# adaLN sums of a hybrid GLA / differential-attention step: groups of blocks in one PSUM bank with one turn each, four blocks per GLA head

## The reference, cut to what matters

```python
def adaln(cond, w, b):                       # w: (1024, 6144), one per layer
    m = jax.nn.silu(cond) @ w + b
    return [t[..., None, :] for t in jnp.split(m, 6, axis=-1)]

for i in range(DEPTH):                       # DEPTH = 2; GLA in layer 0, diff attention in layer 1
    mp = adaln(c_ctx, w_ada[i], b_ada[i])    # for the 128 context tokens
    ms = adaln(c, w_ada[i], b_ada[i])        # for the 512 latent tokens
    hs = rmsnorm(xs, g_mix_norm[i]) * (1 + ms[1]) + ms[0]
    # ... mixer, output os_
    xs = xs + ms[2] * os_
    hs = rmsnorm(xs, g_ffn_norm[i]) * (1 + ms[4]) + ms[3]
    xs = xs + ms[5] * swiglu(hs, w_ffn_gate[i], w_ffn_up[i], w_ffn_down[i])
```

## Time and profile before

| | us |
|---|---|
| median of 3 runs | 1852.03 |
| lowest and highest run | 1846.36, 1852.61 |
| the profiled execution | 1850.31 |
| its span, first to last instruction | 1848.5 |
| TensorE busy | 1745.5 (94%) |
| VectorE busy | 845.4 (46%) |
| ScalarE busy | 704.3 (38%) |
| GpSimd busy | 92.0 (5%) |

### The profile page before, as it was taken

The page is one execution under the profiler, slowest core; times in us unless marked ns, Lnnn a source line. Parts: engine busy times, 40 slices in busy tenths (PEclk is TensorE's granted clock), DMA queues, the critical chain, the costliest instruction groups (busy, mean ns, idle before and its releaser), DMA issues.

```text
span 1848.5 us, 28144 instructions
## 1 busy us (share of the span) xinstructions
PE 1745.5 (94%) x11618; PEld 1632.3 (88%) x11618; DVE 845.4 (46%) x1339; ACT 704.3 (38%) x1055; POOL 92.0 (5%) x139
## 2 busy tenths in 40 slices
PE   5999999979999999999989999996899999999997
PEld 2787787759999999999978999995899999999996
DVE  3434343445444323444356667775464432344433
ACT  5634344324322211222255777776252221122222
POOL 1101021010000000000000000000000000000000
PEclk8999999989999999999989999997999999999998
DMA  9234252332333323323213212222122222222321
GB/s 341 89 128 141 77 196 82 101 109 77 115 114 115 90 70 104 119 75 87 73 43 89 74 55 74 72 57 70 57 69 68 76 89 74 65 72 68 90 69 57
DMA packets 230627, 170.58 MB, mean 92 GB/s; under 512 B 8739, under 2 KB 214982, under 8 KB 229510
## 3 DMA queue, kind: packets, MB, share of 16 engines
q1 hardware_dynamic: 216742, 121.41, 22.4%
q0 software_dynamic: 13792, 47.85, 7.6%
HBM read 160.32 MB, written 4.72 MB: 89 GB/s over the span
## 4 chain that ended last, share of the span: by engine, by line
PE 86%; DVE 5%; ACT 4%; issue 2%; SPq 1%; DMA 1%; POOL 0%; DVEq 0%; ACTq 0%
PE acc L553 71%; PE side L600 2%; PE side L724 2%; PE side L959 2%; PE side L1004 1%; PE work L931 1%; PE acc L1004 1%; DVE state L1726 1%; SPq L378 1%; PE work L741 1%; DVE h_lo L1839 1%; DVE w_lo L1568 1%; PE work L694 1%; ACT w_hi L1077 1%; DMA a_first_x<-in_w_ada_dram 1%
## 5 line engine op out<-in xcount | busy, mean ns | idle before, releaser
L553 PE MATMUL acc<-h_hi,w_hi 128*128 128x320 f32 (+1 forms) x2432 | 584.8, 322 | 27.8 <-DVE h_lo L2087 10.4
L553 PE MATMUL acc<-h_lo,w_hi 128*128 128x320 f32 (+1 forms) x2432 | 559.5, 311 | 0.0
L553 PE MATMUL acc<-h_hi,w_lo 128*128 128x320 f32 (+1 forms) x2432 | 559.2, 311 | 0.0
L553 PEld LDWEIGHTS acc<-h_hi,w_hi 128*128 128x128 f32 x2432 | 410.6, 191 | 60.1 <-issue 34.5
L553 PEld LDWEIGHTS acc<-h_hi,w_lo 128*128 128x128 f32 x2432 | 413.4, 190 | 0.0
L553 PEld LDWEIGHTS acc<-h_lo,w_hi 128*128 128x128 f32 x2432 | 412.4, 190 | 0.0
L1077 ACT ACTIVATE w_hi<-w_raw 128x1024 fp32r<-128x1024 f32 (+1 forms) x184 | 204.1, 1109 | 375.3 <-PE acc L553 369.7
L1568 DVE TENSOR_TENSOR w_lo<-w_raw,w_hi 128x1024 fp32r<-128x1024 f32 (+1 forms) x184 | 237.9, 1293 | 227.6 <-ACT w_hi L1077 225.7
L553 PE MATMUL acc<-hid_lo,w_hi 128*128 128x320 f32 x704 | 160.3, 309 | 0.0
L553 PE MATMUL acc<-hid_hi,w_hi 128*128 128x320 f32 x704 | 160.3, 309 | 0.0
L553 PE MATMUL acc<-hid_hi,w_lo 128*128 128x320 f32 x704 | 160.3, 309 | 0.0
(11 more groups left out here) (271 smaller groups left out, 1747.3 us busy)
## 6 DMA issues: line engine op xcount, KB each, us to landing
a_raw<-in_w_ada_dram POOLq DMA_DIRECT2D x80, 512.0 KB, 6.2
w_raw<-in_w_ffn_gate_dram SPq DMA_DIRECT2D x44, 512.0 KB, 3.8
w_raw<-in_w_ffn_up_dram SPq DMA_DIRECT2D x44, 512.0 KB, 3.8
w_raw<-in_w_ffn_down_dram SPq DMA_DIRECT2D x32, 704.0 KB, 4.6
w_raw<-in_w_gla_in_dram SPq DMA_DIRECT2D x24, 512.0 KB, 4.2
w_raw<-in_w_diff_qkv_dram SPq DMA_DIRECT2D x24, 512.0 KB, 3.9
a_first_h<-in_w_ada_dram SPq DMA_DIRECT2D x5, 1024.0 KB, 11.3
w_raw<-in_w_gla_out_dram SPq DMA_DIRECT2D x8, 512.0 KB, 3.8
```

The costliest lines, as they stand in the source:

```text
L553: mm = pe.matmul(out[:, s, 0:HALF + s * more], w[slot][:, k * P:(k + 1) * P], a(k)[:, s * HALF:(s + 1) * HALF + s * more], start=(k == 0 a ...
```

## The change

- `cond` is widened by 30 zero columns on its left; `cond_at(k, place)` is a window of 32 columns of it. With `place` = n the two conditioning vectors fall on columns 2n and 2n + 1 of the window, so up to 16 blocks can be added into different rows of one bank.
- Blocks form groups: 4 to 19, 20 to 22, and 23. Only the first sum of a group starts the accumulation (and only there TensorE waits for the mods of the group before). Only the last block of a group has a copy, a turn (2 x blocks columns per product) and an add of mods.
- Each head has four blocks, 4h+4 to 4h+7. Their places: behind k = 1 of the Q product (in head 0 this is directly in front of the gates "Zf"), behind k = 5 of the K product (where the first block stood), behind k = 1 of the second V part, and behind k = 6 of the first R part. The turn of block 19 stands in head 3 where the third block's turn stood.
- Block 20 is in the tail, 21 beside unit 0 of the first FFN, and 22 behind that FFN, as 16, 17 and 22 were. The first FFN's other units hold no block and become a loop.
- GpSimd's queue is the same text; with four blocks per head it sends one more load behind the state transfers, and blocks 20 to 22 in the tail.
- `row_pick` has 32 columns; `sq_dump` is laid over the buffers of g1.

```diff
-        ADA_TAIL = 16
-        ADA_FFN = 17
-        ADA_UP = [{3: 18, 6: 19}, {0: 20, 4: 21}]
+        ADA_TAIL = 20
+        ADA_FFN = 21
+        ADA_UP = [{}, {}]
         ADA_NORM2 = 22
         ADA_LAST = 23
+        ADA_GROUPS = [(4, ADA_TAIL - 1), (ADA_TAIL, ADA_NORM2), (ADA_LAST, ADA_LAST)]
+        def ada_ends(b):
+            return ada_group(b)[1] == b
+        def cond_at(k, place):
+            return cond[:, k, CW - 2 * place:CW - 2 * place + CG]
         def ada_blocks_of(h):
-            return [4 + 3 * h + j for j in range(3)]
+            return [4 + 4 * h + j for j in range(4)]
...
             def ada_sums(b, out):
+                lo, hi = ada_group(b)
                 for q in range(4):
                     pe.wait_ge(a_in[q], 16 * (b - 3))
                 for j in range(2):
                     for q in range(4):
-                        mm = pe.matmul(out[q * CG:(q + 1) * CG, 0:512], cond[:, 2 * q + j, :], a_raw[q][:, j, :],
-                                       start=(j == 0), stop=(j == 1))
+                        mm = pe.matmul(out[q * CG:(q + 1) * CG, 0:512], cond_at(2 * q + j, b - lo), a_raw[q][:, j, :],
+                                       start=(b == lo and j == 0), stop=(b == hi and j == 1), skip_group_check=True)
             def ada_block(b):
-                pe.wait_ge(ada_mod, b)
+                if ada_group(b)[0] == b:
+                    pe.wait_ge(ada_mod, b)
                 ada_sums(b, misc).then_inc(ada_mm, 4)
             def ada_turn(b):
+                if not ada_ends(b):
+                    return
                 pe.wait_ge(ada_row, b + 1)
...
+                n = 2 * (hi + 1 - lo)
                 for j in range(4):
-                    mm = pe.matmul(out[:, 2 * j:2 * j + 2], a_row[:, j * P:(j + 1) * P], row_pick[:, :],
+                    mm = pe.matmul(misc[:, n * j:n * (j + 1)], a_row[:, j * P:(j + 1) * P], row_pick[:, 0:n],
                                    start=True, stop=True)
-                return mm
+                mm.then_inc(ada_t, n // 2)
...
-                gaps = {0: old(lambda: kv_sums(h - 1, 1, 0)), 2: old(lambda: kv_sums(h - 1, 1, 1)),
+                gaps = {0: old(lambda: kv_sums(h - 1, 1, 0)), 1: [ada[0]], 2: old(lambda: kv_sums(h - 1, 1, 1)),
...
                 gemm(3 * h, 1, KD, h_hi_k, h_lo_k,
-                     {3: old(lambda: outputs(h, 1)), 5: [ada[0]], 7: [lambda: gates(h, 1, "Zb")]})
+                     {3: old(lambda: outputs(h, 1)), 5: [ada[1]], 7: [lambda: gates(h, 1, "Zb")]})
                 gemm(3 * h + 1, 0, KD, h_hi_k, h_lo_k,
-                     {3: [turns[0]], 7: old(lambda: o_turn(h, 0, "OT0"))})
+                     {7: old(lambda: o_turn(h, 0, "OT0"))})
                 gemm(3 * h + 1, 1, KD, h_hi_k, h_lo_k,
-                     {1: [ada[1]], 3: [lambda: scores(h, 0, "Af")], 7: old(lambda: o_turn(h, 1, "OT1"))})
+                     {1: [ada[2]], 3: [lambda: scores(h, 0, "Af")], 7: old(lambda: o_turn(h, 1, "OT1"))})
                 gemm(3 * h + 2, 0, KD, h_hi_k, h_lo_k,
-                     {1: [lambda: v_turn(h, 0, "VT0")], 2: [turns[1]], 4: [lambda: k_end_turn(h, 0, "Tf")], 6: [ada[2]]})
+                     {1: [lambda: v_turn(h, 0, "VT0")], 4: [lambda: k_end_turn(h, 0, "Tf")], 6: [ada[3]]})
...
-                      5: [lambda: kv_sums(h, 0, 3)], 6: [turns[2], lambda: kv_sums(h, 0, 4)],
+                      5: [lambda: kv_sums(h, 0, 3)], 6: [turns[3], lambda: kv_sums(h, 0, 4)],
```

More of the change, by code:

```diff
@@ L48 @@
 CG = 32
+CW = 30
 GLA_IN = 0
@@ L108, in program @@
         gain = keep("gain", [P, 4, 2, KD])
-        cond = keep("cond", [P, KD, CG])
-        row_pick = keep("row_pick", [P, 2])
+        cond = keep("cond", [P, KD, CG + CW])
+        row_pick = keep("row_pick", [P, CG])
         lam_neg = keep("lam_neg", [P, 1])
@@ L124, in take @@
                 return t
+            take.here = here
             return take
@@ L175, in program @@
         g2 = take("g2", [P, 2, 512])
+        g1_at = take.here[0]
         g1_raw = take("g1_raw", [P, KD, 2 * RANK])
@@ L179, in program @@
         decay = take("decay", [P, 2, NCH])
-        sq_dump = take("sq_dump", [P, DV])
+        sq_dump, _ = at("sq_dump", [P, DV], F32, g1_at)
         take = carve(20 * KB)
@@ L335, in live, with ada_group @@
             return 0 <= h < AH
-        ADA_TAIL = 16
-        ADA_FFN = 17
-        ADA_UP = [{3: 18, 6: 19}, {0: 20, 4: 21}]
+        ADA_TAIL = 20
+        ADA_FFN = 21
+        ADA_UP = [{}, {}]
         ADA_NORM2 = 22
         ADA_LAST = 23
+        ADA_GROUPS = [(4, ADA_TAIL - 1), (ADA_TAIL, ADA_NORM2), (ADA_LAST, ADA_LAST)]
+        def ada_group(b):
+            return next((lo, hi) for lo, hi in ADA_GROUPS if lo <= b <= hi)
+        def ada_ends(b):
+            return ada_group(b)[1] == b
+        def cond_at(k, place):
+            return cond[:, k, CW - 2 * place:CW - 2 * place + CG]
         def ada_blocks_of(h):
-            return [4 + 3 * h + j for j in range(3)]
+            return [4 + 4 * h + j for j in range(4)]
         block = ctx.enter_context(nc.Block())
@@ L599, in ada_sums @@
                     for q in range(4):
-                        mm = pe.matmul(out[q * CG:(q + 1) * CG, 0:512], cond[:, 2 * q + j, :], a_raw[q][:, j, :],
-                                       start=(j == 0), stop=(j == 1))
+                        mm = pe.matmul(out[q * CG:(q + 1) * CG, 0:512], cond_at(2 * q + j, b - lo), a_raw[q][:, j, :],
+                                       start=(b == lo and j == 0), stop=(b == hi and j == 1), skip_group_check=True)
                 return mm
             def ada_block(b):
-                pe.wait_ge(ada_mod, b)
+                if ada_group(b)[0] == b:
+                    pe.wait_ge(ada_mod, b)
                 ada_sums(b, misc).then_inc(ada_mm, 4)
             def ada_turn(b):
+                if not ada_ends(b):
+                    return
                 pe.wait_ge(ada_row, b + 1)
[L612 to L616, removed]
+                pe.wait_ge(pick_ready, 1)
+                lo, hi = ada_group(b)
+                n = 2 * (hi + 1 - lo)
                 for j in range(4):
-                    mm = pe.matmul(out[:, 2 * j:2 * j + 2], a_row[:, j * P:(j + 1) * P], row_pick[:, :],
+                    mm = pe.matmul(misc[:, n * j:n * (j + 1)], a_row[:, j * P:(j + 1) * P], row_pick[:, 0:n],
                                    start=True, stop=True)
-                return mm
+                mm.then_inc(ada_t, n // 2)
             def turn_first(out):
@@ L660, in ada_first @@
                 for b in range(4):
-                    mm = pe.matmul(misc[b * CG:(b + 1) * CG, :], cond[:, k, :], a_first(k)[:, b * 512:(b + 1) * 512],
+                    mm = pe.matmul(misc[b * CG:(b + 1) * CG, :], cond_at(k, 0), a_first(k)[:, b * 512:(b + 1) * 512],
                                    start=(k == 0), stop=(k == KD - 1))
@@ L1118, in ada_rows @@
             def ada_rows(b):
+                if not ada_ends(b):
+                    return
                 act.wait_ge(ada_mm, 4 * b + 4)
-                act.activation(a_row[:, :], misc, ACT.Copy).then_inc(ada_row, 1)
+                act.activation(a_row[:, :], misc, ACT.Copy).then_inc(ada_row, b + 1 - ada_group(b)[0])
             act.wait_ge(vecs_ready, 2)
             act.wait_ge(cond_zero, 1)
-            act.activation(cond[:, :, 0], vecs[:, C_S:C_S + KD], ACT.Silu)
-            act.activation(cond[:, :, 1], vecs[:, C_P:C_P + KD], ACT.Silu).then_inc(cond_ready, 1)
+            act.activation(cond[:, :, CW], vecs[:, C_S:C_S + KD], ACT.Silu)
+            act.activation(cond[:, :, CW + 1], vecs[:, C_P:C_P + KD], ACT.Silu).then_inc(cond_ready, 1)
             for k in range(KD):
@@ L1215, in gla_head @@
                 blocks = ada_blocks_of(h)
-                ada_rows(blocks[0])
                 gate_logs(h, 1, "Zb")
@@ L1225, in gla_head @@
                 decays(h, 1)
-                ada_rows(blocks[1])
                 split_hi(p + 2, 1)
@@ L1231, in gla_head @@
                 split_hi(p + 3, 0)
-                ada_rows(blocks[2])
+                ada_rows(blocks[3])
                 if not first:
@@ L1628, in ada_mods @@
             def ada_mods(b):
[L1629 to L1633, removed]
+                if not ada_ends(b):
+                    return
+                lo, hi = ada_group(b)
+                n = hi + 1 - lo
+                dve.wait_ge(ada_t, hi + 1)
+                dve.tensor_tensor(mods[:, 4 * lo:4 * hi + 4, :].rearrange("p (b j) v -> p b j v", j=4),
+                                  misc[:, 0:8 * n].rearrange("p (j b v) -> p b j v", j=4, v=2),
+                                  mod_bias[:, 4 * lo:4 * hi + 4].rearrange("p (b j) -> p b j", j=4).unsqueeze(3)
+                                  .to_broadcast([P, n, 4, 2]), ALU.add).then_inc(ada_mod, n)
             dve.memset(cond[:, :, :], 0.0).then_inc(cond_zero, 1)
@@ L1643, in _ @@
             dve.wait_ge(const_in, 16)
```

(10 more changed lines are left out.)

## The result

| | us |
|---|---|
| before, median of 4 runs | 1852.3 (1846.36 to 1852.61) |
| after, median of 4 runs | 1872.91 (1869.71 to 1873.82) |
| ratio, 95% interval | 1.0116 (1.0092 to 1.0139) |
| profiled execution after, its span | 1873.82, 1872.0 |

The change costs 20.6 us by the medians, where the forecast was 18.8 us and a time of 1870.

The account below looks back on a forecast made before the run. TensorE's queue, busy 94% of the span, was taken as the bound. Heads 1 to 3 +31.6 us, head 0 -1.3 and first FFN -11.5 gave +18.8 us: 1870 us, with 8 in 10 between 1859 and 1880.

Parts of the forecast that it names:

- The wait, its place and its cause: Heads 1 to 3, second block behind k = 5: its load is sent behind the outputs wait; with clock loss +35.7 us.
- Its size: Wait of 9.9 us in each of heads 1 to 3, with 7.0 us taken from issue to landing of the load.
- The clock: Behind each of three waits in heads 1 to 3 the clock falls to half: 2.0 us each, from 1.5 to 2.6.
- The turns: Turns of blocks on TensorE, 0.81 us each: 6.5 us saved in heads 1 to 3, 4.1 in the first FFN.
- the waits for mods: Heads 1 to 3: TensorE's waits for mods go with the turns, 3 x 1.06 = 3.2 us saved.
- Head 0: Wait of about 3 us at the second block, scores +0.3 us, two turns -1.6: -1.3 us together.
- The tail: Tail block's turn removed: no gain, since 0.81 us more is waited for h_lo behind it.
- The first FFN: Four blocks of sums leave (-7.4 us) and five turns go (-4.1); the loop costs nothing: -11.5 us, stretch 478 us.
- Rival 1: Heads 1 to 3: second block's load is in place, no wait, so faster: -16.9 us, 1834; chance 0.06.
- Rival 2: Heads 1 to 3: slowest part lands in 4.3 us, wait 7.1, clock 1.5: +8.9 us, 1860; chance 0.08.
- rival 3: Landing as in the tail burst: wait 12.3 us, clock 2.6, head 0 +3: sum +30.5 us, 1881; chance 0.10.
- rival 4: Turns were hidden: removing them only lengthens other waits, 10 us of gains gone: +29 us, 1880; chance 0.04.

Follow-up runs that it names:

- Experiment 1: Changed kernel, with the second block's load in heads 1 to 3 sent on GpSimd before the wait for the outputs and the state transfers: 1832.15 us, ratio 0.9909.
- Experiment 4: Kernel before, with only the first block's load of heads 1 to 3 moved behind the wait for the outputs and the state transfers: 1885.26 us, ratio 1.0192.
- experiment 2: Changed kernel, with the second block's load in heads 1 to 3 still behind the wait for the outputs but ahead of the state transfers: 1867.27 us.
- experiment 3: Changed kernel with only the groups kept: three blocks per head and four in the first FFN as in the kernel before: 1831.72 us, ratio 0.991.
- Experiment 7: Experiment 1 plus the forward scores placed behind k = 4, not k = 3, of the second V product: 1829.36 us.
- experiment 5: Experiment 1 plus block 4 summed inside head 0's Q product, behind k = 5: 1828.79 us.
- experiment 6: Experiment 1 plus the load of the tail's block 20 sent before the stores of head 3's final states: 1832.41 us.
- experiment 8: Experiment 1 plus the edits of experiment 5, experiment 6 and Experiment 7 together: 1824.07 us, ratio to before 0.9869.

## Why the prediction held, step by step

| stretch | before | after | measured | forecast |
|---|---|---|---|---|
| head 0 (gates or first block to head 1) | 84.4 | 84.7 | +0.3 | +0.6 |
| head 1 | 80.98 | 93.42 | +12.4 | +10.3 |
| head 2 | 80.96 | 92.57 | +11.6 | +10.3 |
| head 3, tail, projection | 144.2 | 156.8 | +12.7 | +9.2 |
| first FFN | 489.4 | 476.9 | -12.5 | -11.5 |
| the rest | 968.6 | 967.6 | -1.0 | 0 |

(The stretches of head 1 and 2 end at the same product as in the earlier trace rows. The forecast column is the sum of the prediction by place. A stretch begins behind its head's Q product, so the new first block of heads 1 to 3, +1.9 each, lies in the stretch before: head 0 is -1.3 + 1.9, head 3 is 11.1 - 1.9.)

The mechanism held, and the closeness of the total is in part luck. Against the forecast the three waits with their clock took 4.0 us more, new waits in front of the scores 3.6, and a low clock in the projection 2.3; the tail's block took 2.6 less, the first FFN 1.0 and the rest 1.0. The spans end 4.7 us over the forecast. The medians end only 1.8 over it, since the profiled execution before lies 2.0 us under its median and the one after 0.9 over its own.

- **The wait, its place and its cause: right.** Three of 11.1, 10.5 and 12.0 us. Experiment 1 takes them away and gives 40.8 us back; their sum is 33.7 us and the half clock 2.0 each, 39.7 together. Experiment 4 puts them into the kernel before.
- **Its size: 9.9 us forecast, 11.2 measured.** The term that was too small is the landing, 7.0 us taken, 8.4 on average. The four parts, the states and one weight load are 3.15 MB that now start together, where the load before ran mostly after the other two. That they share one bandwidth would explain it: from 155 to 161 all transfers of the core together move 360 to 430 GB/s, their order didn't matter to the slowest part in experiment 2, and without the states the slowest part lands after 7.2 us on average in experiment 1. No run changed the bytes alone, so this stays argued. The fit of the Trainium skill (DMA: Bandwidth & Descriptors, Anatomy of one DMA — SWDGE (gpsimd) path) gives, as an estimate, 3.2 us for one part of 512 KB. These bursts don't bear it out: their fastest parts took 5.9 to 7.5 us. The page gives the fit per DMA, and no run here shows such a part without the other three. The prediction's "no part landed faster than 4.3 us" holds for the three bursts of the earlier trace rows; the fastest of all 80 parts before took 4.0.
- **The clock: right.** 3.64 - 1.86 = 1.8 us on the block, and the first pair of the next product costs some 0.25 more (167.17 to 167.83 is 0.66 us, where such a pair to pair distance is 0.40): 2.0. From the start of the block to the gates "Zb" it is 5.69, 5.39 and 6.05 us in heads 1 to 3, where it was 3.71: 2.0, 1.7 and 2.3 us, 6.0 in all as forecast.
- **The turns: right; the waits for mods: wrong.** The first FFN with all its five blocks and no turns (experiment 3) takes 484.9 us for 489.4, 0.9 for each of five turns where 0.81 was taken, and experiment 3 shows that it was no hidden time. But the 3.2 us of waits for mods, which the sum took as gone, came back as 3.6: 1.2 us in each of heads 1 to 3 in front of the scores. Between the gates "Zb" and the scores the turn and the wait for mods had lain, 1.9 us of queue; with them gone the chain of ScalarE and VectorE down to the gated output (15.5 us from gates to its end, in both kernels) is longer than what TensorE has in between. The prediction had no term for this. Experiment 7 shows that such a wait is only uncovered time: a product put in front of it takes 0.9 of the 1.2 us away.
- **Head 0: right.** Forecast were a wait of about 3 us, gates at 77.7 and scores between 90.7 and 92.4, which the trace misses by 0.3. TensorE after, first block, second block, gates, scores, which answers to the earlier trace rows:

```profile
61.12 1.92 PE L617 MATMUL side<-a_raw,cond 128*32 128x512 f32 x16 [0.84 <-ACT z L1160]
...
72.72 3.33 PE L617 MATMUL side<-a_raw,cond 128*32 128x512 f32 x16 [3.15 <-DMA a_raw<-in_w_ada_dram]
...
77.84 1.24 PE L701 MATMUL work<-z,g 128*128 128x320 f32 x4
...
92.73 1.27 PE L721 MATMUL work<-q_d,k_d 128*128 128x128 f32 x10
```

- **The tail: its turn was worth nothing, as said.** The wait for h_lo grew from 0.92 to 1.71 us, by the 0.8 us of the turn. Not foreseen: the wait for the load was shorter (1.60 for 2.75 us) and the clock stayed full at the block, some 2.6 us better. Nor was it foreseen that 2.3 us of this are lost again behind it: from the row of h_lo to the block in the first FFN it is 64.1 us, before 61.8.

```profile
430.31 1.92 PE L617 MATMUL side<-a_raw,cond 128*32 128x512 f32 x16 [1.60 <-DMA a_raw<-in_w_ada_dram]
...
441.77 0.90 PE L569 MATMUL acc<-h_hi,w_hi 128*128 128x320 f32 x2 [1.71 <-DVE h_lo L1826]
```

The clock behind that row, columns as in the earlier trace rows, in the kernel after, before, and in experiment 3, which has the same two waits of 1.07 and 1.71 us in front of it:

```profile
441.80:446.90 5.10, 5.10 (x19) 5.10 (x20) 0.97 (x3) 0.00 (x0) 0.00 (x0) 0.50 0.00 1
...
407.00:411.40 4.40, 4.40 (x20) 4.40 (x20) 0.95 (x3) 0.00 (x0) 0.00 (x0) 0.61 0.00 1
...
393.00:398.00 5.00, 3.74 (x24) 3.48 (x24) 1.91 (x4) 1.06 (x1) 0.00 (x0) 1.00 0.00 0
```

In the ten traces this stretch takes 60.2 to 64.1 us (60.2 in experiment 3, 64.1 in the kernel after) with the same work in it. Experiments 1 and 5 have the same queue on TensorE here and take 61.6 and 60.3. So one profile against another can differ by up to 3.9 us here alone, as much as experiments 5 and 7 changed. What decides it is open.

- **The first FFN: right.** The chain of waits at the same two points as the earlier trace rows: 476.85 us, forecast 478. The loop costs nothing: experiment 3, written out, takes 484.9 with four blocks more (7.4 us), so the loop comes out 0.6 cheaper.

```profile
488.65 1.23 DVE w_lo L1586
...
965.50 1.15 DVE x L1849 x3
```

- **Rival 1** had its number right and its condition wrong: without the waits the kernel takes 1832.15 us, 1834 was worked out. Rival 2 is out, since the slowest parts landed after 7.7 to 9.2 us and not 4.3, and rival 3, since the time is 1872.91 and not 1881, though head 3's wait of 12.0 us came near its 12.3. For rival 4 the 17.9 us of experiment 3 are the evidence.

## What to carry to other kernels

A block moved to an earlier place in one engine's queue needs its load earlier too: lay the queue that sends the loads beside the one that uses them, and count from the last thing the sender waits for. Here the arithmetic savings were real but for 1.2 us per head, and one order in GpSimd's queue turned some 18 us of gain into some 20 us of loss. And when waits and small work disappear from a stretch, ask how long the chain beside it is, for that is what it can't get shorter than.

## What was not expected

- A longer wait cost no more clock: at the blocks, waits of 2.6 to 3.8 us were followed by sums of 3.2 to 3.6 us, and waits of 9 to 12 us as well. Waits of 1.1 to 2.3 us in front of the tail's block left it at 1.92 us. But the length of the last wait doesn't settle it: behind the same waits of 1.07 and 1.71 us the projection began at the half clock in the kernel after and in experiments 1 and 2 (first pair 0.90 us), and at the full one in experiments 3, 5, 6, 7 and 8 (0.56 us).
- The same burst of four loads of 512 KB landed its slowest part after 6.1 us in one place and after 9.2 us in another. What else was under way at the time is the likely reason, but it isn't shown apart from the rest.
